# Turning the attention weights by ordinary float32 matmuls with the identity instead of TensorE's transpose mode

## What is computed

```python
def _diff_attend(q, k, v, lam):
    s = jnp.einsum('bhcqd,bhckd->bhcqk', q, k, preferred_element_type=jnp.float32) * (A_DQK ** -0.5)
    p = jax.nn.softmax(s, axis=-1)
    w = p[:, :, 0] - lam * p[:, :, 1]
    return jnp.einsum('bhqk,bhkd->bhqd', w.astype(v.dtype), v)
```

## Time and profile before

| what | value |
|---|---|
| median of 3 runs | 3718.29 us (3709.38 to 3722.48) |
| the profiled execution, its own time | 3710.92 us |
| its span, first to last instruction | 3709.1 us |
| TensorE matmuls, share of the span | 87% |
| VectorE, ScalarE, GpSimd | 50%, 28%, 8% |
| granted TensorE clock, mean over the span | 0.881 of full speed |
| turnings of the weights (line 650) | 656 |

### The profile page before, as it was taken

The page is one execution under the profiler, slowest core; times in us unless marked ns, Lnnn a source line. Parts: engine busy times, 40 slices in busy tenths (PEclk is TensorE's granted clock), DMA queues, the critical chain, the costliest instruction groups (busy, mean ns, idle before and its releaser), DMA issues.

```text
span 3709.1 us, 45803 instructions
## 1 busy us (share of the span) xinstructions
PE 3221.3 (87%) x17774; PEld 1859.2 (50%) x17774; DVE 1846.1 (50%) x2565; ACT 1045.0 (28%) x1514; POOL 301.9 (8%) x208
## 2 busy tenths in 40 slices
PE   6798778777889999999999489679787899999997
PEld 6344544566454665555545234445666444444443
DVE  1794745788447211222225595746776364122235
ACT  2311213444344111111113311214444353111122
POOL 2400000000121000000002230000000210000001
PEclk8999669566889999999999699778666999999998
DMA  4110010011112321111111100011111222111112
GB/s 182 48 41 17 6 36 35 35 45 45 50 53 89 115 91 63 40 36 44 40 51 63 56 35 35 6 42 46 57 57 40 80 90 103 51 50 47 51 57 102
DMA packets 59451, 206.87 MB, mean 56 GB/s; under 512 B 7360, under 2 KB 8384, under 8 KB 59328
## 3 DMA queue, kind: packets, MB, share of 16 engines
q1 hardware_dynamic: 58176, 199.89, 15.1%
q10 hardware_dynamic: 1152, 5.24, 0.4%
HBM read 200.91 MB, written 4.19 MB: 55 GB/s over the span
## 4 chain that ended last, share of the span: by engine, by line
PE 54%; issue 26%; DVE 13%; ACT 5%; POOL 1%; DMA 0%; SPq 0%; POOLq 0%; DVEq 0%; ACTq 0%
PE PS L555 49%; DVE R L1578 4%; DVE wlo L1317 2%; PE PS L740 1%; ACT X L1031 1%; ACT R L1029 1%; DVE R L1395 1%; PE PS L613 1%; DVE R L1382 1%; ACT whi L984 1%; POOL st L1945 1%; PE PS L796 1%; DVE R L1700 1%; PE PS L586 1%; DVE X L1674 0%
## 5 line engine op out<-in xcount | busy, mean ns | idle before, releaser
L555 PE MATMUL PS<-R,whi 128*128 128x512 f16 (+1 forms) x7808 | 2131.5, 360 | 121.8 <-DVE wlo L1317 50.1
L555 PE MATMUL PS<-R,wlo 128*128 128x512 f16 (+1 forms) x3904 | 1404.7, 360 | 0.0
L555 PEld LDWEIGHTS PS<-R,whi 128*128 128x128 f16 x7808 | 765.8, 99 | 902.8 <-issue 68.7
L1317 DVE SCALAR_TENSOR_TENSOR wlo<-stage,whi 128x1024 f16<-128x1024 f32 (+1 forms) x260 | 332.0, 1277 | 513.5 <-ACT whi L984 495.7
L555 PEld LDWEIGHTS PS<-R,wlo 128*128 128x128 f16 x3904 | 385.2, 99 | 382.2 <-issue 17.8
L984 ACT ACTIVATE whi<-stage 128x1024 f16<-128x1024 f32 (+1 forms) x260 | 268.7, 1034 | 183.5 <-PE PS L555 133.6
L1876 POOL TENSOR_TENSOR X<-X 128x512 f32<-128x512 f32 (+2 forms) x105 | 154.6, 1475 | 1755.7 <-ACT X L1248 1611.2
L1578 DVE SCALAR_TENSOR_TENSOR R<-X,small,R 128x1024 f32<-128x1024 f32 (+1 forms) x180 | 219.1, 1267 | 1.8
L1816 DVE SCALAR_TENSOR_TENSOR X<-X,PS 128x512 f32<-128x512 f32 (+3 forms) x60 | 62.0, 1034 | 305.6 <-PE PS L555 305.5
L650 PE MATMUL PS<-ident,R 128*128 128x128 f32 x656 | 146.9, 374 | 74.1 <-DVE R L1440 46.9
L1811 DVE SCALAR_TENSOR_TENSOR X<-X,PS 128x512 f32<-128x512 f32 (+3 forms) x60 | 62.1, 1035 | 297.5 <-ACT X L1265 297.5
(11 more groups left out here) (183 smaller groups left out, 2517.6 us busy)
## 6 DMA issues: line engine op xcount, KB each, us to landing
stage<-in_w_gu SPq DMA_DIRECT2D x120, 512.0 KB, 3.4
X<-in_w_ada SPq DMA_DIRECT2D x60, 512.0 KB, 3.5
stage<-in_w_down SPq DMA_DIRECT2D x48, 512.0 KB, 3.5
stage<-in_w_in SPq DMA_DIRECT2D x44, 512.0 KB, 3.5
stage<-in_w_out SPq DMA_DIRECT2D x32, 512.0 KB, 3.5
T<-in_w_ada SPq DMA_DIRECT2D x20, 512.0 KB, 3.5
R<-in_w_ada SPq DMA_DIRECT2D x16, 512.0 KB, 10.4
stage<-in_w_down SPq DMA_DIRECT2D x16, 384.0 KB, 2.9
```

The lines of the kernel that those rows point to most:

```text
L555: last = mm(slot(j, t0, t1)[:, c0 - t0:c1 - t0], w[:, j, k, :], row, start=(k == 0 and q == 0), stop=(k == K - 1 and q == 2))
L1317: STT(wlo[:, j, 0:K, :], stage[:, j, 0:K, :], WS, whi[:, j, 0:K, :], ALU.mult, ALU.subtract).then_inc(S["w_lo"], 1)
```

## The change

`turn` in the program of TensorE calls the ordinary matmul in place of the transpose. The stationary operand is the block of `Wt`, the moving one the identity, both float32; the output, its place in PSUM, the order of the calls, the waits and the semaphore that the last block of a group raises all stay. Every engine's program holds the same rows in the same order before and after. The other users of transpose mode (lines 810, 880, 925) and `turn_out` are unchanged.

```diff
                     o = turned(p, m * P)
                     for i in range(m):
-                        last = nc.tensor.transpose(o[:, i * P:(i + 1) * P],
-                                                   Wt[h % 2][:, (k0 + i) * P:(k0 + i + 1) * P], ident[:, :])
+                        last = mm(o[:, i * P:(i + 1) * P], Wt[h % 2][:, (k0 + i) * P:(k0 + i + 1) * P], ident[:, :],
+                                  start=True, stop=True)
                     last.then_inc(s("wt_ps"), 1)
```

## The result

The changed kernel takes 3759.14 us in the median of 4 runs (3753.11 to 3763.86), the kernel before 3715.44 us on the same chips (4 runs). The ratio is 1.0124 with a 95% interval of 1.0107 to 1.0141: slower by 44 us. A later run of both gave 1.0111 (1.0095 to 1.0127), 41 us. The forecast was 3767 us, slower.

What follows compares the result with a forecast made beforehand. No engine was full in latent attention; a loop through TensorE, ScalarE and VectorE set the time, with the turning on it. 3710.9 + 53 (16 latent tiles) + 3.4 (context) = 3767 us; 8-in-10 range 3702 to 3808.

Steps and rivals of the forecast that it cites:

- 0.213 and 0.112 us for one more: TensorE time of the record added per turned block: 0.213 us at 1.2 GHz, 0.112 us at 2.4 GHz.
- The lower bound of the price: At 1.2 GHz an added record costs at least 0.213 us, from modulation matmul spacing; the upper bound was 0.43 us.
- place 0: Layer 1 tile, head burst from 2710.76: between +0.35 us (clock kept at 2.4 GHz) and +1.7 us (1.2 GHz); taken +0.55 us.
- Context: Context tiles, two blocks a head, low clock, VectorE waiting for the copy: 8 x 2 x 0.213 = 3.4 us added.
- The four places: The four head bursts of a layer 1 tile, priced one by one: together 3.3 us more per tile.
- Place 3: Layer 1 tile, burst from 2702.44: group 0 slow, groups 1 and 2 start 0.55 us late, group 1 adds 0.43: +0.97 us.
- Place 1: Layer 1 tile, burst from 2719.34: values 0.75 us late, extra of groups 1 and 2 hidden behind VectorE: +0.75 us.
- place 2: Layer 1 tile: group 0 adds 0.85 us, rising clock returns 0.25, group 1 adds 0.43: +1.03 us.
- I take layer 0 the same: Layer 0 latent tiles get the same 3.3 us each as layer 1; 16 tiles in all, 53 us.
- The faster one: Rival: added latent attention work keeps TensorE's clock up, -0.3 us a head, -19 us plus 3 for context: 3695 us; chance 14%.
- The full price at the low clock: Rival: clock stays at 1.2 GHz, each latent head pays 1.7 us, 109 us in all: 3823 us; chance 9%.
- hidden after all: Rival: TensorE's idle gaps in the latent stretches take up the additions, leaving 3711 + 3 = 3714 us; chance 8%.

Runs made afterwards that it cites:

- group 0 alone: Against the kernel before, only the first turned group of each head uses ordinary matmuls, the later two stay in transpose mode: 3751.95 us, ratio 1.0085.
- the wide fillers: Kernel before plus three useless float16 matmuls of 512 columns ahead of group 0 in latent tiles, where TensorE waits for `combine`: 3696.00 us, ratio 0.9932.
- the two halves of the change: Kernel before with ordinary matmuls only for group 0 (3751.95 us, ratio 1.0085), or only for groups 1 and 2 (3701.51 us, ratio 0.9950).
- doubled transposes: Kernel before with every block turned twice in transpose mode, 1312 records: 3732.01 us, ratio 1.0036; repeated, 3734.18 us, ratio 1.0061.

## Why the prediction was right, and where its steps were off

**What bounds the kernel.** Right: VectorE's wait for the copies was the number that moved (40.1 to 75.1 us in layer 1, 25.6 to 51.8 us in layer 0), and the loss lies in the three attention stretches.

**Two records for a block.** Right: 1312 records. **0.213 and 0.112 us for one more.** Right inside a group. Missing was 0.1 us at the head of each group at 1.2 GHz (0.05 to 0.07 at 2.4): eight records are 2.07 us, where 1.11 + 0.85 = 1.96 was forecast. The 4x of the Trainium skill (TensorE: Matmul & The Clock Gate, Terms), by which the sum would have been three times as large, doesn't come out of these records: a block is two of them in place of one, and each is as far apart as a transpose is. The lower bound of the price held. One term of the working was off: for place 0 at 2.4 GHz I took eight records as 8 x 0.107 + 0.17 = 1.03 us, where the earlier trace rows and my own spacing give 0.66 + 4 x 0.112 = 1.11 us; they measured 1.16 us. So even at the higher clock group 0 would not have come out cheaper than the 1.11 us of before.

**Context.** Forecast +3.4, measured +4.3 us. The context group of four records shows the same head cost; before (first row), and now (second):

```profile
646.80 0.69 PE L650 MATMUL PS<-ident,R 128*128 128x128 f32 x2 [1.09 <-DVE R L1440]
```

```profile
649.77 1.22 PE L650 MATMUL PS<-ident,R 128*128 128x128 f32 x4 [1.09 <-DVE R L1440]
```

which is +0.53 in place of +0.43 us a head, 8 times.

**The four places.** Their sum for a tile in layer 1 was right, 3.3 against 3.4 us, and 26.4 against 26.1 us for the stretch, but by compensation. Three of the four terms failed, each by a microsecond or more. Place 0: "I take +0.55 us, near the lower end". The clock stayed low until the middle of groups 1 and 2, and the step paid close to its upper bound, 1.64 of 1.7 us. Place 3: +0.97 was entered and +2.03 came, since the clock rose 1.5 us after the start of groups 1 and 2 where it had risen 0.3 us after it before. Place 1: +0.75 was entered and -1.07 came, the gain. Only place 2 was about right (1.03 and 0.83).

That the sum still came out is luck, and the traces show how much of it. Many tiles keep to one of a few lengths. In layer 1 the length is 37.5 us in five of seven tiles of the kernel before (37.48 to 37.54), and 41.0 us in three of seven of the changed kernel and in five of seven of its second run (40.91 to 40.97). With group 0 alone it is 40.9 to 41.0 us in six of seven already, so there groups 1 and 2 add almost nothing to it (333.2 and 334.4 us for the stretch). With the wide fillers in the kernel before it is 37.4 to 37.6 us in six tiles of layer 1, and 34.1 to 34.2 us in five of layer 0. GpSimd's rows with group 0 alone (first) and with the fillers, layer 0 (second):

```profile
2796.04 1.01 POOL L1953 TENSOR_TENSOR st<-st,tiny 128x4 f32<-128x4 f32 x1 [39.93 <-DVE st L1456]
```

```profile
855.42 1.01 POOL L1955 TENSOR_TENSOR st<-st,tiny 128x4 f32<-128x4 f32 x1 [33.13 <-DVE st L1458]
```

A sum of four terms came to 3.3 us where the loop went from one length that it often keeps to the next, 3.4 us on.

**"I take layer 0 the same."** This term was mis-sized: 26.4 us forecast, 14.2 measured. The clock rose further there (0.82 against 0.77), and the two halves of the change act on each other in layer 0 alone. Layer 0 has fewer modulation matmuls in a tile; whether that is the reason, no run tests.

**The rivals.** The faster one was right in its mechanism and wrong in what it was weighed against: the clock did rise, to near the top of the range that I gave (0.67 to 0.80) in layer 1 and past it in layer 0. With group 0 left in transpose mode it pays for the whole of groups 1 and 2 and 18 us more. Group 0, four blocks that nothing hides, costs 33 us by itself, and with it in the new form groups 1 and 2 no longer pay either. The full price at the low clock (3823 us) is off by far; hidden after all (3714 us) as well. The rule of the Trainium skill (TensorE: Matmul & The Clock Gate, Part 4) that transposes don't count for the clock doesn't hold here: with them doubled the clock was 0.82 and 0.76 in place of 0.67.

**The size.** The sum was +56.4 us, attention gave +44.6 in the profile, and the medians differ by 44 us: 12 us too much, nearly all of it the term of layer 0. The forecast of 3767 was only 8 us high, since it started from an execution that lay 4.5 us under the median; that part is luck too.

**The profile after.** As listed: 1312 records, stages outside attention unchanged, VectorE's wait above 60 us. Off: the longest record (582 ns, not 480), group 0 at 1.2 GHz (2.07 us, not about 1.9), and layer 0 (308 us, not 318, which was itself 3 us less than 295 + 26.4).

What stays open: some 10 us of the difference between doubled transposes and ordinary matmuls, why the two halves of the change don't add up in layer 0, and why a tile settles at one length and not at another. No run isolates these.

## What to carry to other kernels

Where TensorE sits at 1.2 GHz inside a loop with another engine, the price of added TensorE work has two signs: ask for each piece whether it lies on the loop or in a gap, and what the clock does to all the other pieces. Measure the pieces in pairs and not only one by one: here the halves gave +33 and -18 us and the whole +44. Take the waits of the engine that closes the loop as a sign of direction, and not TensorE's busy share: here 2-column fillers raised the busy time and left the clock where it was. A cheap test is a few wide, useless matmuls in a gap: if they make a kernel faster, the clock was part of the cost.

## What was not expected of the hardware

- Work whose result is thrown away makes this kernel faster by 0.7% (ratio 0.9932), by lifting the granted clock in latent attention from 0.67 to 0.82 and 0.77.
- The same place filled with 2-column matmuls makes it slower by 1.2% (ratio 1.0121), with the clock at 0.67 and 0.65.
- A group of ordinary float32 matmuls costs 0.1 us more than one of doubled transposes at 1.2 GHz (2.07 and 1.97 us for eight records), once for each group.
- In several of these kernels most tiles of a latent stretch have one length, and it is 34.1, 37.5 or 41.0 us, though the kernels differ in their work; in others the lengths lie between.
- The same program gave latent stretches of 302.0 and 332.3 us in one execution and 293.4 and 320.7 us in another (doubled transposes). A single profile of such a loop is a sample.
